# A mixture-of-experts step on one core: the last block of expert rows given to one expert, some of the final reads asked for before the last write

## The reference

```
sel, wts = top-8 of 64 experts for each token (4 of 8 groups allowed), weights normalised x 2.5
for each expert e:   y[t, e] = wt * ((silu(h[t] @ Wg[e]) * (h[t] @ Wu[e])) @ Wd[e])
yf = sum of the 8 y rows of a token + (silu(h @ Sg) * (h @ Su)) @ Sd      # shared expert
x  = x1 + gate * rms_norm(yf) * g
```

## Time and profile before

| | |
|---|---|
| median of 3 runs | 1107.8 us (1106.04 to 1108.03) |
| the profiled execution: its time / its span | 1108.23 us / 1106.4 us |
| PE (TensorE) busy | 1065.5 us, 96% of the span |
| DVE (VectorE) busy | 729.2 us, 66% |
| ACT (ScalarE) busy | 215.3 us, 19% |
| POOL busy | 136.3 us, 12% |
| moved by DMA | 337.11 MB, mean 305 GB/s |

### The profile page before, as it was taken

One profiled execution on the slowest core, in us unless ns is written; L12 is line 12 of the kernel. 1 busy time (PEld: TensorE's weight loads), 2 busy tenths in 40 slices (PEclk: granted clock), 3 DMA queues, 4 the chain that ended last, 5 costly groups with the idle time before them and its releaser, 6 DMA issues.

```text
span 1106.4 us, 16559 instructions
## 1 busy us (share of the span) xinstructions
PE 1065.5 (96%) x5954; PEld 535.9 (48%) x5954; DVE 729.2 (66%) x1934; ACT 215.3 (19%) x473; POOL 136.3 (12%) x163
## 2 busy tenths in 40 slices
PE   6999999999999999999999999999899999999797
PEld 3456678777877644664333333333233333333242
DVE  3218441546546645766988888888687987888148
ACT  4131332222233313301111111111011110111111
POOL 0110000000020010111121211111112111121100
PEclk9999999999999999999999999999999999999999
DMA  9958720120352277769999999999999999999798
GB/s 368 339 197 301 244 81 24 53 86 1 115 190 87 77 242 248 293 283 380 409 413 425 424 425 424 422 424 427 422 425 424 423 424 420 412 416 406 255 425 334
DMA packets 51653, 337.11 MB, mean 305 GB/s; under 512 B 9636, under 2 KB 14088, under 8 KB 30830
## 3 DMA queue, kind: packets, MB, share of 16 engines
q1 hardware_dynamic: 33710, 287.32, 64.2%
q0 software_dynamic: 17856, 48.68, 11.6%
HBM read 311.30 MB, written 37.24 MB: 315 GB/s over the span
## 4 chain that ended last, share of the span: by engine, by line
PE 79%; DMA 12%; DVE 5%; ACT 2%; issue 1%; SPq 0%; DVEq 0%; ACTq 0%
PE bank L1594 23%; PE bank L1617 12%; PE bank L1289 10%; DMA mem<-in_w_exp_down 6%; PE bank L1308 5%; PE bank L1407 3%; DMA hT<-in_w_exp_down 3%; PE bank L1408 3%; PE bank L1525 3%; PE bank L1202 3%; PE bank L1286 3%; DMA mem<-in_w_sh_down 2%; PE bank L1703 2%; PE bank L1177 1%; DVE mem L2290 1%
## 5 line engine op out<-in xcount | busy, mean ns | idle before, releaser
L1594 PE MATMUL bank<-mem 128*32 128x512 f32 (+2 forms) x1568 | 334.0, 595 | 1.8 <-DVE mem L2290 1.0
L2290 DVE STREAM_TRANSPOSE mem<-mem 32x256 f32<-32x256 f32 x448 | 195.1, 436 | 5.8
L1617 PE MATMUL bank<-mem 128*32 128x512 f32 (+2 forms) x712 | 178.4, 608 | 10.9 <-DMA mem<-in_w_exp_down 7.0
L1594 PEld LDWEIGHTS bank<-mem 128*32 128x32 f32 (+2 forms) x1568 | 106.9, 128 | 164.9 <-issue 164.9
L1289 PE MATMUL bank<-hT,mem 128*128 128x288 f32 x512 | 133.3, 409 | 1.0 <-ACT mem L968 1.0
L2290 DVE STREAM_TRANSPOSE mem<-x_sb 32x256 f32<-32x256 f32 x240 | 104.5, 435 | 3.1
L1289 PEld LDWEIGHTS bank<-hT,mem 128*128 128x128 f32 x512 | 93.8, 190 | 25.8 <-issue 2.4
L1617 PEld LDWEIGHTS bank<-mem 128*32 128x32 f32 (+2 forms) x712 | 56.8, 133 | 81.4 <-issue 71.1
L1594 PE MATMUL bank<-x_sb,mem 128*32 128x512 f32 (+2 forms) x256 | 87.1, 596 | 0.0
L2306 DVE COPY hT<-bank 128x512 f32<-128x512 f32 x48 | 33.1, 691 | 67.2 <-PE bank L1617 67.1
L822 POOL DMA_INDIRECT mem<-ffn_in_rows,idxg x32 | 32.9, 1030 | 268.0 <-DVE idxs L2274 192.6
(11 more groups left out here) (404 smaller groups left out, 1218.9 us busy)
## 6 DMA issues: line engine op xcount, KB each, us to landing
mem<-k_w_exp SPq DMA_DIRECT2D x54, 2048.0 KB
mem<-in_w_exp_down SPq DMA_DIRECT2D x52, 1024.0 KB
x_sb<-k_w_exp SPq DMA_DIRECT2D x10, 2048.0 KB
mem<-k_w_ada SPq DMA_DIRECT2D x8, 2048.0 KB, 9.2
mem<-k_w_in SPq DMA_DIRECT2D x7, 2048.0 KB, 9.0
hT<-in_w_exp_down SPq DMA_DIRECT2D x12, 1024.0 KB
mem<-expert_out_rows SPq DMA_DIRECT2D x6, 2048.0 KB, 15.7
mem<-k_w_head SPq DMA_DIRECT2D x4, 2048.0 KB, 17.3
```

Source lines behind the costliest of these rows:

```text
L1594: i = mm(bank[sl, :], xT[:, j % 2, c * BLK + sl.start:c * BLK + sl.stop], gu_view(r)[:, c, :], start=c == 0, stop=c == KC - 1)
L1617: i = mm(ps[4 + hf][sl, :], hhT[:, k * BLK + sl.start:k * BLK + sl.stop], dn_view(r)[:, k, hf * 512:(hf + 1) * 512], start=k == 0, stop=k ...
L2290: i = dve.transpose(cols[dl, :, sl], rows[sl, :, dl])
```

## The change

The tables `CAPS` and `PRE` are new. The last rank now always is expert 63, with four units, and it is alone in the last block. So the last scatter writes only rows of expert 63, which are the last of the 8 rows of their token, since these lie in the order of the expert numbers; the first four rows of any token are complete when block 46's scatter has landed. Three reads are issued at that point: the sample's first half (1 MB) and the first four rows of tiles 1 and 2 (2 MB each). The sample's second half is asked for once all scatters have landed, then the other reads as before. The five-place ring is numbered anew, since the sample takes one number less. The shared down weights are asked for before the residual rows. Three small parts handle the overflow case.

```diff
-PRE = [0, 1, 4, 5]
-CAPS = [4, 4, 2, 2, 4, 4, 2, 2, 2, 2, 4, 5, 3, 4, 3, 5, 2, 2, 3, 1,
-        6, 3, 3, 2, 5, 2, 3, 4, 1, 3, 2, 2, 4, 4, 2, 3, 3, 3, 2, 3, 5, 3, 4, 3, 3, 2, 3, 2,
-        3, 7, 3, 2, 4, 4, 3, 2, 3, 2, 2, 4, 2, 2, 1, 3]
+PRE = [0, 1, 4, 24]
+CAPS = [4, 4, 2, 2, 4, 3, 2, 3, 3, 5, 2, 2, 3, 3, 6, 2, 2, 4, 2, 2,
+        4, 2, 2, 5, 4, 3, 4, 4, 4, 2, 2, 3, 1, 3, 5, 3, 1, 3, 3, 3, 3, 5, 6, 1, 4, 4, 4, 2,
+        2, 3, 3, 3, 3, 4, 2, 2, 2, 3, 3, 2, 2, 2, 2, 4]
...
-RANK = [PRE.index(r) if r in PRE else 0 for r in range(len(CAPS))]
-for i_, r_ in enumerate(sorted((r for r in range(len(CAPS)) if r not in PRE), key=lambda r: -CAPS[r])):
+RANK = [PRE.index(r) if r in PRE else 0 for r in range(len(CAPS) - 1)] + [len(CAPS) - 1]
+assert LASTB.count(NBK - 1) == 1 and CAPS[-1] * QS == BLK
+for i_, r_ in enumerate(sorted((r for r in range(len(CAPS) - 1) if r not in PRE), key=lambda r: -CAPS[r])):
...
-    first = np.where(e < len(PRE), (len(PRE) - e) * 2 ** 17, 0)
+    first = np.where(e < len(PRE), (len(PRE) - e) * 2 ** 17, 0) - np.where(e == NE - 1, 2 ** 17, 0)
```

On SP, between the last weights and the reads of the end:

```diff
+            sp.wait_ge(S["eup"], last_use(EXTSLOT) + 1)
+            load_down(sp, dn_s, A["w_sh_down"][0], S["ld_br"])
             sp.wait_ge(S["eup"], last_use(XSLOT) + 1)
             sp.wait_ge(S["xT_ready"], NBK)
             for t in range(NT):
                 sp.dma_start(x_sb[0:ROWS[t], t, :], x1_d[t * P:t * P + ROWS[t], :]).then_inc(S[f"ld_x{t}"], 16)
-            sp.wait_ge(S["eup"], last_use(EXTSLOT) + 1)
-            load_down(sp, dn_s, A["w_sh_down"][0], S["ld_br"])
...
+            def y_sample(k, s):
+                sp.dma_start(yhalf[k:P:2, 0, :], yv[SEQ:T, KPE * k * D:KPE * (k + 1) * D]).then_inc(S[s], 16)
+
+            EARLY = [1, 3]
...
+            sp.wait_ge(S["eup"], NBK)
+            sp.wait_ge(S["sct0"], 16 * (NBK // 2))
+            sp.wait_ge(S["sct1"], 16 * (NBK // 2 - 1))
+            y_sample(0, "yh0")
+            for q in EARLY:
+                y_rows(q, COMBINE[(q + 1) // 2][0], 0, KPE, f"yh{q}")
             nov = overflow_count(sp)
             sp.wait_ge(S["edn"], NBK)
...
             for k in range(2):
                 sp.wait_ge(S[f"sct{k}"], 16 * (NBK // 2))
...
-            for k in range(2):
-                sp.dma_start(yhalf[k:P:2, 0, :], yv[SEQ:T, KPE * k * D:KPE * (k + 1) * D]).then_inc(S[f"yh{k}"], 16)
+            y_sample(1, "yh6")
             for i, (t, _) in enumerate(COMBINE):
                 for k in range(2 if i else 0):
-                    q = 2 * i + k
-                    if q == NYH:
-                        sp.wait_ge(S["yd_sum"], 1)
-                    elif q > NYH + 1:
-                        sp.wait_ge(S["yd_sum" if (q - NYH) % 2 else "yp_mm"], (q - NYH) // 2 + 1)
+                    q = 2 * i - 1 + k
+                    if q in EARLY:
+                        continue
+                    if q >= NYH:
+                        sp.wait_ge(S["yp_mm" if (q - NYH) % 2 else "yd_sum"], (q - NYH + 1) // 2 + 1)
```

On VectorE, before the sample's sum:

```diff
-                    for k in range(2):
-                        dve.wait_ge(S[f"yh{k}"], ycount(k))
+                    dve.wait_ge(S["yh0"], 16)
+                    dve.wait_ge(S["yh6"], 16)
```

More of the change, by code:

```diff
@@ L680, in _, with y_rows @@
                 sp.dma_start(x_sb[0:ROWS[t], t, :], x1_d[t * P:t * P + ROWS[t], :]).then_inc(S[f"ld_x{t}"], 16)
-            sp.wait_ge(S["eup"], last_use(EXTSLOT) + 1)
-            load_down(sp, dn_s, A["w_sh_down"][0], S["ld_br"])
+            yv = y_d.rearrange("(t k) d -> t (k d)", k=TOPK)
+            def y_rows(q, t, k0, k1, s):
+                at_ = (k0 - (q + 1) % 2 * KPE) * D
+                sp.dma_start(yhalf[0:ROWS[t], q % NYH, at_:at_ + (k1 - k0) * D], yv[t * P:t * P + ROWS[t], k0 * D:k1 * D]).then_inc(S[s], 16)
+            def y_sample(k, s):
+                sp.dma_start(yhalf[k:P:2, 0, :], yv[SEQ:T, KPE * k * D:KPE * (k + 1) * D]).then_inc(S[s], 16)
+            EARLY = [1, 3]
+            assert DN_PLACE[NE - 1] not in (1, 3)
+            sp.wait_ge(S["eup"], NBK)
[4 more added lines that the diff above has]
+                y_rows(q, COMBINE[(q + 1) // 2][0], 0, KPE, f"yh{q}")
             nov = overflow_count(sp)
@@ L691, in body, with early_landed @@
                 load_dn(NE + j, e)
+            def early_landed():
+                for q in [0] + EARLY:
+                    sp.wait_ge(S[f"yh{q}"], 16)
             def last_rows():
@@ L697, in last_rows @@
                 sp.sem_inc(S["over"], 1)
-            overflow(sp, nov, body, last=last_rows)
+                y_sample(0, "ld_br")
+                for q in EARLY:
+                    y_rows(q, COMBINE[(q + 1) // 2][0], 0, KPE, "ld_br")
+            overflow(sp, nov, body, early_landed, last_rows)
             sp.wait_ge(S["xT_ready"], NBK)
@@ L721, in _ @@
                         y_rows(q, t, KPE // 2, KPE, f"yh{q % NYH}")
-            y_rows(2 * LAST + 1, t, KPE, TOPK - 2, f"yh{(2 * LAST + 1) % NYH}")
-            y_rows(2 * LAST + 1, t, TOPK - 2, TOPK - 1, "yh5")
-            y_rows(2 * LAST + 1, t, TOPK - 1, TOPK, "yh6")
+            y_rows(2 * LAST, t, KPE, TOPK - 2, f"yh{2 * LAST % NYH}")
+            y_rows(2 * LAST, t, TOPK - 2, TOPK - 1, "yh5")
+            y_rows(2 * LAST, t, TOPK - 1, TOPK, "yh6")
             for i, (t, _) in enumerate(COMBINE):
@@ L1687, in last_done @@
                 pe.sem_inc(S["over"], 1)
+                pe.wait_ge(S["ld_br"], 16 * 4)
             overflow(pe, nov, body, first_blocks, last_done)
@@ L1712, in _ @@
                 t, kp = COMBINE[o]
-                n, q = ROWS[t], 2 * o
+                n, q = ROWS[t], 2 * o - 1
                 if o < LAST:
@@ L1725, in _ @@
                         mm(ps[2 * (o % 4) + hf][0:n, :], ident[0:n, 0:n], yhalf[0:n, (q + 1) % NYH, D + hf * 512:D + (hf + 1) * 512], start=False, stop=False)
-                    pe.wait_ge(S["yh6"], 16)
+                    pe.wait_ge(S["yh6"], 32)
                     for hf in range(2):
@@ L2350, in first_blocks, with last_read @@
                 idx_out(NBK + 1, NBK + 1)
-            overflow(dve, nov, body, first_blocks)
+            def last_read():
+                dve.wait_ge(S["ld_br"], 16 * 4)
+            overflow(dve, nov, body, first_blocks, last_read)
             dve.wait_ge(S["ld_bc"], 4 * SPREAD + 16)
@@ L2372, in own_sum @@
                     dve.wait_ge(S["x2_done"], i - 1)
-                q = 2 * i + 1
+                q = 2 * i
                 if i < LAST:
```

## The result

The changed kernel takes 1113.84 us in the median of four runs (1112.32 to 1115.03), the kernel before in the same comparison 1106.92 us (1105.53 to 1108.03). The ratio is 1.0065, with a 95% interval of 1.0052 to 1.0078: 0.65% slower. The profiled execution took 1115.03 us with a span of 1113.2 us, 6.8 us more than the span before.

The account below looks back on a forecast made before the run. Blocks: PE and transfers nearly equal; then VectorE's chain from the sample tile bounds the tail. 1108.23 + 5.7 (VectorE past the sample at 1072.3, not 1066.63) + 0 (tables) = 1113.9, median 1113.5 us; range 1107 to 1118.

Parts of the forecast that it names:

- The order of the queue: Sample tile's reads: the second half queues behind two large reads, 6.3 MB instead of 2.1 MB, 14.6 us instead of 4.9.
- The formula of first issue + 2.9 us + bytes / 431 GB/s: Sample reads after the blocks: gives the second half's landing, forecast at 1064.6 us.
- Rival 1: Sample's second half shares the engines with the large reads, landing at 1058.0; -2.8 us, 1105 us; chance 11%.
- The moment of the early reads: After block 46's scatter: first early read issued at 1047.1 instead of 1049.05, a gain of 2 us.
- Rival 2: Block 46's scatter is complete early, at 1043.9; 3.2 us less than the sum, 1108.4 to 1110.3 us; chance 15%.
- PE's clock: Sample's pairs on PE: after 9 us without work they run at 1.2 GHz, 3.8 us instead of 1.88.
- The tables: Blocks: waits on down weights move to blocks 9, 16 and 25; taken as 0, bounds -3 and +5 us.
- Rival 3: Blocks lose: the place held by expert 3's weights lets the queue run dry early; +5, 1118.5 us; chance 14%.
- rival 4: Tables win up to 3 us at blocks 24 to 36 and the queue ends earlier; 1110.5 us, within the range.
- The shared down weights: Tail: asked for earlier, by itself worth up to 5.7 us; worth nothing with the sample's sum at 1068.4.
- landed by 1094 if none waits for its place: End of the tail: six remaining half reads, 12.6 MB or 29 us, land before VectorE's last product near 1108.
- The sum: Profiled execution: 1108.23 + 5.7 + 0 = 1113.9 us; the median 0.4 lower, 1113.5 us.

Follow-up runs that it names:

- experiment 2: The changed kernel with the sample's first half and tile 1's rows read early, tile 2's not: 1109.42 us, ratio 1.0016 to the kernel before.
- experiment 1: The changed kernel with only the sample's first half read early, no large read: 1107.09 us, ratio 0.9998 to the kernel before.
- experiment 8: The changed kernel with the residual rows (2.4 MB) asked for behind the sample's second half: 1114.13 us, ratio 1.0068 to the kernel before.
- experiment 6: The changed kernel with two more shared products, thrown away, to keep PE busy until the pairs: 1113.20 us, ratio 1.0048 to the kernel before.
- experiment 4: The kernel before with the new tables alone, its own reads and requests: 1107.67 us, ratio 1.0006.
- experiment 3: The kernel before with one edit, shared down weights asked for ahead of the residual rows: 1107.41 us, ratio 1.0004.
- 7: The changed kernel with only the sample's first half early and the residual rows behind its second half: 1113.88 us, ratio 1.0054 to the kernel before.
- 12: The changed kernel with only the sample's first half and tile 1's first two rows early, and another block order: 1108.45 us, ratio 1.0009 to the kernel before.

## Why the prediction was right, point by point

**The order of the queue.** Forecast: the second half lands 13 to 16 us after its issue; measured 14.8 (1050.99 to its use at 1065.85). The formula of first issue + 2.9 us + bytes / 431 GB/s gives 17.5 us for the changed kernel and 12.6 for experiment 2; from the first issue to VectorE's start it was 18.0 (1047.83 to 1065.85) and 12.9 (1047.99 to 1060.89). It does not hold everywhere: experiment 1 took 12.0 us where it gives 7.8, and experiment 8 21.3 us where it gives 17.5, in both of which the second half was issued late; experiment 6, otherwise like the changed kernel, took 19.4 us. Rival 1, the second half sharing the engines with the reads before it, would have had it there at 1058 and falls.

**The moment of the early reads.** Forecast 1047.1, measured 1047.83; over the six traces with the same blocks and the residual rows ahead 1046.5 to 1048.1. Rival 2, scatter 46 complete 4.5 us after its issue, falls for this kernel. Its mechanism is real, as experiment 8 shows (3.4 us), but needs a queue without the residual rows. Most of what it would bring there is lost again to the last scatter (11.1 us), a link that the prediction did not have: it counted the last scatter at nothing, as issued before the early reads.

**PE's clock.** Forecast 3.8 us for the pairs after an idle PE, measured 3.68 at a granted clock of 0.50; experiment 6 shows that the idle time makes it (1.93 us at 1.00). The idle time itself was forecast as 9 us and is 8.93. But the shared products did not start at 1045 without a wait: they started at 1046.61 after 2.96 us, whose cause is open. It cost nothing, as PE had 8.93 us to spare.

**The tables.** Forecast 0 with bounds of -3 and +5, with waits at blocks 9, 16 and 25 and none at 24, 29 and 36. They came there, as far as the profile names them (see above), and one more at block 14 that I had not named. The blocks lose about 2.4 us, of which experiment 4 leaves 0.6 us (-0.3 to +1.7) at the end. Rival 3 (+5) and rival 4 (-3) both fall. That part of it would be hidden since the queue's remainder depends on bytes was said, and fits the moment of the early reads, which does not follow the scatter's.

**The shared down weights.** Here the prediction was wrong, without weight in the sum. "By itself this would be worth up to 5.7 us" took the tail to be VectorE's alone. It was too much by its own rows, too: VectorE has the sample's sum at 1060.6 and PE's pairs began at 1064.66, so no more than 4.1 us could be won. PE did gain 2.0 us on the pairs in experiment 3, and the kernel nothing. Two things were missed. The start of the shared products moved by 1.7 us only, and they still took 16.73 us: PE was idle for 4.33 us before them, and in each microsecond from 1045 to 1050 the granted clock is 0.50. Above all, the reads of tiles 1 to 4 run so close behind VectorE that 2 us of gain meet waits for rows [experiments 1, 3, 4, 7]. My estimate that the reads would be "landed by 1094 if none waits for its place" counted without these places: in the changed kernel the last read goes out at 1089.3, and none lands in less than 8.0 us. It did no harm there, as VectorE is late and never waits for rows after the sample.

**The sum.** Forecast +5.7 us on the profiled execution, measured +6.8: the first read 0.7 us later than taken, 0.5 us more from there to VectorE's start (18.0 against 17.5), and 0.1 less for the pairs. The largest of these differences is no larger than the spread between traces (1.6 us in the moment of the first read). The medians moved by 6.9 us, from 1106.92 to 1113.84; that the forecast of 1113.5 is only 0.3 us off is in part luck, since it was added to 1107.8.

The terms are the right ones, as 1, 2 and 6 each take one of them away. The second large read is worth 5.4 us (1.0065 - 1.0016 of 1107 us) where 4.9 were forecast for the queue and the pairs take 0.6 us less (3.06 against 3.68); the clock is worth 1.8 us on the pairs. Both large reads together are worth 7.4 us (1.0065 - 0.9998) and not the 10.7 us that I expected for experiment 1: the last scatter was complete late there, and the second bound took the rest.

## What to carry to other kernels

Before a read is issued early, write down what will be queued behind it, and price the bytes that now stand ahead of the piece that is needed first; here 4.2 MB ahead of a 1 MB read cost more than the 1.2 us that the early issue won. A small write that others wait for can be held up by what the engines still have to move and by large reads issued just ahead of it, as in experiment 8. When an engine's chain moves and the time does not, look for waits on transfers further down: behind a bound that is 2 us shorter here stood the next.

## What the runs showed of the hardware

- How long a scatter takes from its issue to the issue of the reads that wait for it depends on what else the DMA engines have. Block 46: by 3.4 and 3.8 us without the residual rows in the queue (experiments 8 and 7), 5.2 to 7.7 us with them. Block 47: 4.1 to 5.7 us in the five kernels that read nothing early, 4.1 to 6.9 us where the early reads went out after it, 11.1 us with 5.2 MB of reads issued ahead of it (experiment 8). In the kernels before and after the mean busy share of the engines was 0.11 and 0.12 in 1045 to 1046, which fits a few engines being late; no view here shows the engines one by one, and why some would lag is open.
- Four small products took 1.93 us after 0.34 us without work (experiment 6) and after 1.32 us (7), 3.06 us after 3.86 us (2), 3.14 us after 2.27 us (12), and 3.68 us after 8.93 us in the changed kernel.
- After the last block PE starts the shared products of the changed kernel after 2.96 us that no transfer or engine explains; in experiment 3 it is 4.33 us. In experiments 7, 8 and 12 it is 1.19 us, put down to VectorE's last copy. In 7 and 8 no residual rows were in the queue, in 12 they were, but its last block ended 2 us later. What the longer waits are for is not shown; it was not tried apart.
